# Where TensorE sums the values and turns the probabilities in the dilated attention of a two-block kernel

## The chip, the cores and the metric

The kernel runs on one core of one Trainium2 chip. The metric is device time in microseconds (us) of one execution, as the median of several runs. Engines are named as in the profile: PE is TensorE (matmuls and transposes), PEld its weight load, DVE is VectorE, ACT is ScalarE, POOL is GpSimd, SP is SyncE, which issues the weight loads from memory.

## What is computed

Two transformer blocks on 512 tokens of width 1024, in f32. Only the first block's attention is touched by the change. It is a dilated attention of 12 heads of 64 channels, beside a pooling branch of 256 channels:

```python
for window, dilation in ((128, 1), (512, 4), (2048, 16)):
    o, lse = dilated_branch(q, k, v, window, dilation)
w = softmax(stack(lses)); attn = sum(w * outs)
pool = (mean of the last 2, 4, 8 or 16 tokens - u) @ w_pool * pool_scale
x = x + rms_norm(concat([pool, attn]) @ w_out)
```

The kernel computes the three branches as one causal softmax: a bias table holds the logarithm of the number of branches that see a key, so each head needs one matrix of scores, one of probabilities and one product with the values. Queries and keys are rotated (rope) first.

## The kernel before

All activations are held with channels on partitions and the 512 tokens along the free axis. A weight tile of 128 output channels is a **unit**. It is used in three products: the weights are split into a high part WH (copied by ACT, `split_hi`, line 336) and a low part WL (subtracted by POOL, line 595), the input into HH and HL. `high_part` (lines 355 and 356) issues 8 x 2 matmuls of 128x512, WH with HH and with HL. `low_part` (line 364) issues 8 more, WL with HH. These run in a rounded f32 format; scores, turns and values are plain f32 matmuls.

The heads are taken in six pairs. `attn_stage(j, a)` on each engine does the projections of pair j (units u, u+1, u+2: queries, keys, values) and the attention of pair a = j - 1; the last call has no j and takes the first units of the output projection (`some_out`, lines 391 to 393) in the place of the projections. "The stage of pair a" means this call. Every engine runs its instructions in the order in which they are written, and they meet through semaphores. The order on PE in the stage of pair a, before the change:

- `scores()`, line 900: 8 matmuls into banks 2 to 6. Waits for the rotated queries and keys of the pair (`a_qk`) and, for a > 0, for all copies of turned probabilities of pair a-1 (`a_pt_act`, `a_pt_dve`).
- `turn_v()`, line 940: 4 transposes of the pair's values into bank 1.
- the first unit into bank 0 (`high_part`, `low_part`).
- `values(a - 1)`, line 931: 8 matmuls of probabilities with values of the pair before into bank 7.
- the second unit into bank 1.
- `turn(0)`, line 916: 10 transposes of head 0's probabilities PR into banks 2, 3 and 4, which signal three times.
- `high_part` of the third unit, which waits for the pair j's rotated queries (`a_qk`, since it writes bank 0).
- `turn(1)`: the same for head 1 into banks 5, 6 and 4. It waits until DVE has copied both of head 0's pieces (`a_pt_dve`), since both heads use bank 4.
- `low_part` of the third unit, and in the stages of pairs 1 and 3 (`POOL_ENDS`) `pool_product`, line 879, which waits for the pooling differences DF of DVE (`p_d`).

What stands on the other engines, in order, is not touched. On DVE: mask head 0, mask head 1 (line 2181), normalise head 0 (2190, 2194), the query's cosine product (2145), normalise head 1, the query's rotation (2149, 2153), the low half of the mixed values (2165), in pairs 1 to 3 two running sums of the pooling (2115), and then

```python
                    times_cos(1)
                if a is not None and j is not None:
                    copy_probs(0)
                ...
                    if a in POOL_ENDS:
                        pool_averages(POOL_ENDS[a])
                    rotate(1)
                    if a in POOL_ENDS:
                        pool_differences(POOL_ENDS[a])
                if a is not None:
                    copy_probs(1)
                if j is not None:
                    scale_v()
```

`copy_probs(h)` takes two pieces of a head out of the banks (lines 2201 and 2203), `pool_averages` is line 2130, `pool_differences` line 2133, `scale_v` line 2159. On ACT: `copy_v` (1596, waits for `turn_v`), the exponentials of head 0 (1576), the split of unit u+2, the exponentials of head 1, four copies that swap the query's halves (1584), the high half of the mixed values (1569), the split of u+3, the swap of the key's halves, head 0's third piece (1591), the split of u+4, head 1's third piece, and in pairs 1 and 3 the scaled pooling result. POOL makes the low weights of the next unit as soon as an old one is done.

Of the kernel before, what the change touches and what calls it, by code (L numbers as in the profile page):

```python
# [76 lines left out]
def t_width(block):  # L77
    return T - P * block


def s_width(block):
    return P * (block + 1)
# [46 lines left out]
def build(nc, ins, out_t):  # L129
    ctx = ExitStack()  # L130
    with ctx:
# [127 lines left out]
        POOL_ENDS = {1: 0, 3: 1}  # L259
# [88 lines left out]
        def high_part(pe, u, bank, chunks, xh, xl, k0=0, start=True, halfway=None, at=DC // 2):  # L348

            wh = WH[u.s]  # L350
            pe.wait_ge(s_hi, u.index + 1)
            for c in range(chunks):
                if halfway is not None and c == at:
                    halfway()
                pe.matmul(bank, wh[:, c, :], xh[:, k0 + c, :], start=(start and c == 0), stop=False)  # L355
                mm = pe.matmul(bank, wh[:, c, :], xl[:, k0 + c, :], start=False, stop=False)  # L356
            mm.then_inc(s_hi_used, 1)

        def low_part(pe, u, bank, chunks, xh, k0=0, stop=True):

            wl = WL[u.s]
            pe.wait_ge(s_lo, u.index + 1)
            for c in range(chunks):
                mm = pe.matmul(bank, wl[:, c, :], xh[:, k0 + c, :], start=False,  # L364
                               stop=(stop and c == chunks - 1))
            mm.then_inc(s_unit, 1)
# [284 lines left out]
        def _(pe):  # L651
            def mean_of_sum(n):

                if n == 0:
                    pe.wait_ge(s_sq_used, DC)
                    pe.matmul(B[7][:], MEAN[:], ACC[:], start=True, stop=True).then_inc(s_mean, 1)
                    return

                pe.wait_ge(s_mean_r, 1)
                pe.wait_ge(s_sum_lo, MEANS[n] - 1)  # L660
                pe.matmul(B[7][:], MEANR[:], ACCH[:], start=True, stop=False)
                pe.matmul(B[7][:], MEANR[:], ACCL[:], start=False, stop=True).then_inc(s_mean, 1)
# [198 lines left out]
            def some_out(b, which):  # L861

                if 0 in which:

                    if b == 0:
                        pe.wait_ge(a_vs, PAIRS1)
                    else:
                        pe.wait_ge(a_v, PAIRS1)
                some_chunks(pe, Unit(U_OUT1 + b), B[b][:], which, M1H, M1L, ready_m1)

            def finish_out(b):
                finish_unit(pe, Unit(U_OUT1 + b), B[b][:], DC, M1H, M1L, ready_m1)

            def pool_product(t):

                pe.wait_ge(p_d, t + 1)

                pe.wait_ge(s_m, PAIR_DONE[2 * t])
                pe.matmul(B[7][:], WPOOL[:, t, :], DF[:, t, :], start=True, stop=True).then_inc(p_y, 1)

            def attn_stage(j, a):

                u = None if j is None else Unit(U_ATTN + 3 * j)
                first = j == 0
                first_a = a == 0
                ap = None if a is None else a % 2

                def scores():

                    pe.wait_ge(a_qk, a * 2 + 2)  # L890
                    if not first_a:
                        pe.wait_ge(a_pt_act, a * 2)
                        pe.wait_ge(a_pt_dve, a * 4)
                    for h, tb, bank, at in ((0, 1, 4, 0), (1, 3, 5, 0), (0, 3, 2, 0), (1, 2, 6, 0), (0, 2, 3, 0),
                                            (1, 1, 4, 256), (0, 0, 3, 384), (1, 0, 6, 384)):
                        w = s_width(tb)
                        r = slice(64 * h, 64 * h + 64)
                        if h == 1 and bank == 4:
                            pe.wait_ge(a_scores, a * 8 + 1)
                        pe.matmul(B[bank][:, at:at + w], QT1[r, ap, P * tb:P * tb + P], KT1[r, ap, 0:w],  # L900
                                  start=True, stop=True).then_inc(a_scores, 1)

                def turn(h):
                    hd = a * 2 + h
                    pe.wait_ge(a_probs, hd * 4 + 4)
                    if h == 0:
                        pe.wait_ge(a_masked, a * 8 + 8)
                    else:
                        pe.wait_ge(a_pt_dve, hd * 2)
                    full, rest = ((2, 3), (5, 6))[h]  # L910
                    for blocks in (((0, full, 0),), ((1, rest, 0), (3, rest, 384)), ((2, 4, 256 * h),)):
                        for sb_, bank, at in blocks:
                            for tb in range(sb_, TB):
                                col = S_AT[tb] + P * sb_
                                o = at + P * (tb - sb_)
                                mm = pe.transpose(B[bank][:, o:o + P], PR[:, h, col:col + P], IDENT[:])
                        mm.then_inc(a_turned, 1)

                def values(a, ap):

                    pe.wait_ge(a_pt_act, a * 2 + 2)
                    pe.wait_ge(a_pt_dve, a * 4 + 4)
                    pe.wait_ge(a_v, a + 1)
                    if a in POOL_ENDS:
                        pe.wait_ge(p_yt, POOL_ENDS[a] + 1)
                    elif a:
                        pe.wait_ge(s_m, PAIR_DONE[a - 1])
                    for sb_ in range(TB):
                        w = t_width(sb_)
                        for h in range(2):  # L930
                            mm = pe.matmul(B[7][64 * h:64 * h + 64, P * sb_:T], VN1[:, ap, sb_, 64 * h:64 * h + 64],  # L931
                                           PT[:, h, T_AT[sb_]:T_AT[sb_] + w], start=(sb_ == 0),
                                           stop=(sb_ == TB - 1), skip_group_check=True)
                    mm.then_inc(a_pv, 1)

                def turn_v():
                    pe.wait_ge(a_vs, a + 1)
                    pe.wait_ge(a_qk, a * 2 + 2)
                    for tb in range(TB):
                        mm = pe.transpose(B[1][:, P * tb:P * tb + P], V1[:, P * tb:P * tb + P], IDENT[:])  # L940
                    mm.then_inc(a_vt, 1)

                if a is not None:
                    scores()
                    turn_v()
                if j is not None:
                    if not first:
                        pe.wait_ge(a_vs, j)
                    high_part(pe, u, B[0][:], DC, HH, HL)
                    if first:  # L950
                        pe.wait_ge(s_const, 16 * N_CONST)
                        mean_of_sum(0)
                    low_part(pe, u, B[0][:], DC, HH)
                if a is not None:
                    if not first_a:
                        values(a - 1, 1 - ap)
                    if j is None:
                        some_out(0, range(0, 5))
                        turn(0)
                        some_out(0, range(5, 6))  # L960
                        some_out(1, range(0, 1))
                        turn(1)
                        some_out(0, range(6, 7))
                        some_out(1, range(1, 2))
                        values(a, ap)
                        some_out(1, range(2, 5))
                        finish_out(0)
                        some_out(1, range(5, 7))
                        finish_out(1)
                if j is not None:  # L970
                    if not first:
                        pe.wait_ge(a_v, j)
                    use_unit(pe, u + 1, B[1][:], DC, HH, HL)
                    if a is not None:
                        turn(0)
                    pe.wait_ge(a_qk, j * 2 + 1)
                    high_part(pe, u + 2, B[0][:], DC, HH, HL)
                    if a is not None:
                        turn(1)
                    low_part(pe, u + 2, B[0][:], DC, HH)  # L980
                    if a in POOL_ENDS:
                        pool_product(POOL_ENDS[a])
# [25 lines left out]
            for j in range(1, PAIRS1):  # L1008
                attn_stage(j, j - 1)
            attn_stage(None, PAIRS1 - 1)  # L1010


# [1626 lines left out]
```

## Time and profile before

| | before |
|---|---|
| median of 3 runs | 1965.98 us (1965.83 to 1966.38) |
| span of the profiled execution | 1964.0 us |
| PE busy | 1957.2 us, 100% of the span |
| DVE busy | 865.8 us, 44% |
| ACT busy | 801.4 us, 41% |
| POOL busy | 764.9 us, 39% |
| granted clock of TensorE, mean | 1.000 |

The profile's span ends with the last instruction; the median of the runs is 2.0 us longer. The attention of the first block lies between about 37 and 173 us. A row of the timeline gives the start in us, the busy time in us, the engine, the line, the operation, what it writes and reads, and how many instructions are merged in it; in brackets stands the idle time before it and what ended that. Consecutive matmuls overlap in the records, so how long a group holds PE is read from its start to the start of what follows.

### The profile page before, as it was taken

How to read it: one execution, taken by the hardware profiler on the slowest of the kernel's cores; microseconds unless marked ns; L12 is line 12 of the kernel's file. 1: busy time of each engine (PE TensorE's matmuls, PEld its weight loads, DVE VectorE, ACT ScalarE, POOL GpSimd, SP SyncE). 2: the span in 40 equal slices, each digit the busy share in tenths (PEclk: the TensorE clock that was granted, in tenths of full speed). 3: DMA queues.
4: the chain of work that ended last, by engine and by line, in shares of the span. 5: the costliest groups of instructions: out<-in, count | busy, mean ns of one | idle time of the engine just before them, and what ended most of it. 6: DMA issues, size and time to landing. Idle time of an engine off the chain costs nothing.

```text
span 1964.0 us, 25749 instructions
## 1 busy us (share of the span) xinstructions
PE 1957.2 (100%) x8959; PEld 1590.7 (81%) x8959; DVE 865.8 (44%) x1148; ACT 801.4 (41%) x1078; POOL 764.9 (39%) x307
## 2 busy tenths in 40 slices
PE   9999999999999999999999999999999999999999
PEld 6777888888888778787888888888777788888887
DVE  5775653433145335333243434224788763433200
ACT  6665533233243433324332223225888752323211
POOL 4223344444413334243444444443222244444443
PEclk9999999999999999999999999999999999999999
DMA  5212122223223222222232223222111122222332
GB/s 172 75 65 86 65 97 96 96 96 115 91 74 123 70 86 91 69 87 85 86 105 98 96 96 102 99 99 85 54 63 46 63 97 96 96 96 96 110 97 93
DMA packets 49013, 177.39 MB, mean 90 GB/s; under 512 B 5569, under 2 KB 6465, under 8 KB 48961
## 3 DMA queue, kind: packets, MB, share of 16 engines
q1 hardware_dynamic: 46656, 172.95, 26.3%
q10 hardware_dynamic: 2304, 3.74, 0.6%
q8 instruction: 34, 0.56, 0.1%
q14 instruction: 19, 0.15, 0.0%
HBM read 174.57 MB, written 2.10 MB: 90 GB/s over the span
## 4 chain that ended last, share of the span: by engine, by line
PE 98%; DVE 1%; ACT 0%; DMA 0%; issue 0%; SPq 0%; DVEq 0%; ACTq 0%
PE B L355 26%; PE B L356 26%; PE B L364 26%; PE B L1114 2%; PE B L1251 2%; PE B L1072 1%; PE B L1076 1%; PE B L1073 1%; PE B L381 1%; PE B L377 1%; PE B L376 1%; PE B L1240 1%; PE B L1296 1%; PE B L1158 1%; PE B L900 1%; PE B L931 1%
## 5 line engine op out<-in xcount | busy, mean ns | idle before, releaser
L595 POOL TENSOR_TENSOR WL<-RAW,WH 128x1024 fp32r<-128x1024 f32 (+1 forms) x296 | 753.9, 2549 | 1171.5 <-PE B L364 763.8
L355 PE MATMUL B<-HH,WH 128*128 128x512 f32 x1608 | 629.1, 391 | 0.3 <-DVE QT L2153 0.3
L356 PE MATMUL B<-HL,WH 128*128 128x512 f32 x1608 | 626.1, 389 | 0.0
L336 ACT CAST WH<-RAW 128x1024 fp32r<-128x1024 f32 (+1 forms) x300 | 329.1, 1098 | 555.6 <-PE B L356 475.0
L364 PE MATMUL B<-HH,WL 128*128 128x512 f32 x1608 | 398.3, 390 | 0.0
L355 PEld LDWEIGHTS B<-HH,WH 128*128 128x128 f32 x1608 | 301.8, 188 | 64.9 <-issue 1.7
L364 PEld LDWEIGHTS B<-HH,WL 128*128 128x128 f32 x1608 | 301.4, 188 | 63.2 <-POOL WL L595 0.4
L356 PEld LDWEIGHTS B<-HL,WH 128*128 128x128 f32 x1608 | 301.9, 188 | 62.4
L1921 DVE TENSOR_TENSOR U<-B,RB 128x512 f32<-128x512 f32 x66 | 45.6, 691 | 294.3 <-PE B L364 294.3
L355 PE MATMUL B<-MH,WH 128*128 128x512 f32 x440 | 171.2, 389 | 0.0
L356 PE MATMUL B<-ML,WH 128*128 128x512 f32 x440 | 171.2, 389 | 0.0
L1924 DVE TENSOR_TENSOR HD<-SG,U 128x512 f32<-128x512 f32 x66 | 148.7, 2253 | 7.4 <-ACT SG L1414 0.7
L1418 ACT CAST MH<-HD 128x512 f32 (+1 forms) x66 | 41.0, 621 | 247.0 <-DVE HD L1924 247.0
L1904 DVE TENSOR_TENSOR ACC<-ACC,SQ 128x512 f32<-128x512 f32 x38 | 75.0, 1973 | 114.9 <-ACT SQ L1392 114.8
L1939 DVE TENSOR_TENSOR X<-X,B 128x512 f32 x26 | 17.9, 687 | 216.0 <-PE B L364 195.5
L364 PE MATMUL B<-MH,WL 128*128 128x512 f32 x429 | 103.6, 389 | 0.0
L356 PEld LDWEIGHTS B<-ML,WH 128*128 128x128 f32 x440 | 82.6, 188 | 17.2
L355 PEld LDWEIGHTS B<-MH,WH 128*128 128x128 f32 x440 | 82.6, 188 | 17.1
L364 PEld LDWEIGHTS B<-MH,WL 128*128 128x128 f32 x429 | 80.5, 188 | 16.7
L1414 ACT ACTIVATE SG<-G 128x512 f32<-128x512 f32 x66 | 41.8, 633 | 87.6 <-DVE G L1919 87.6
L1927 DVE TENSOR_TENSOR ML<-HD,MH 128x512 f32 (+1 forms) x66 | 49.4, 748 | 58.3 <-ACT MH L1418 58.3
L1919 DVE TENSOR_TENSOR G<-B,RB 128x512 f32<-128x512 f32 x66 | 45.6, 691 | 54.5 <-PE B L364 45.9
(377 smaller groups left out, 2257.9 us busy)
## 6 DMA issues: line engine op xcount, KB each, us to landing
RAW<-in_w_small SPq DMA_DIRECT2D x254, 512.0 KB, 3.3
RAW<-in_w_large SPq DMA_DIRECT2D x48, 704.0 KB, 4.1
out_t<-X SPq DMA_DIRECT2D x7, 256.0 KB, 5.2
X<-in_x_t ACTq DMA_DIRECT2D x4, 256.0 KB, 6.2
X<-in_x_t SPq DMA_DIRECT2D x4, 256.0 KB, 6.5
DECAY<-in_decay ACTq DMA_DIRECT2D x4, 256.0 KB, 2.6
RAW<-in_w_small ACTq DMA_DIRECT2D x2, 256.0 KB, 6.5
RAW<-in_w_small SPq DMA_DIRECT2D x2, 256.0 KB, 7.4
```

The source lines that it names most:

```text
L336: act.copy(wh, raw).then_inc(s_hi, 1)
L355: pe.matmul(bank, wh[:, c, :], xh[:, k0 + c, :], start=(start and c == 0), stop=False)
L356: mm = pe.matmul(bank, wh[:, c, :], xl[:, k0 + c, :], start=False, stop=False)
L364: mm = pe.matmul(bank, wl[:, c, :], xh[:, k0 + c, :], start=False, stop=(stop and c == chunks - 1))
L595: pool.tensor_tensor(wl, raw, wh.bitcast(F32), ALU.subtract).then_inc(s_lo, 1)
L1414: act.activation(SG[:], G1[:], ACT.Silu).then_inc(s_silu, 1)
L1418: act.copy(MH[:, i, :], HD[:]).then_inc(s_m_hi, 1)
L1904: dve.tensor_tensor(ACC[:], ACC[:], SQ[b][:], ALU.add).then_inc(s_sq_used, 1)
L1919: dve.tensor_tensor(G1[:], gate, RB[:], ALU.mult).then_inc(s_gate, 1)
L1921: dve.tensor_tensor(U1[:], up, RB[:], ALU.mult).then_inc(s_up, 1)
L1924: dve.tensor_tensor(HD[:], SG[:], U1[:], ALU.mult).then_inc(s_hidden, 1)
L1927: dve.tensor_tensor(ML[:, i, :], HD[:], MH[:, i, :].bitcast(F32), ALU.subtract).then_inc(s_m, 1)
```

## The change

Two groups of PE instructions move; none is added or removed, and no other engine's order changes. In the stages of pairs 1, 3 and 5, `values(a - 1)` moves from behind the first unit (in pair 5's stage: from behind `turn_v`) to directly behind `scores()`. In pairs 2 and 4 it stays, since there bank 7 holds the pooling product. And in the stages of pairs 0 to 4 `turn(0)` moves from ahead of the third unit's high part to behind it, directly ahead of `turn(1)`.

```diff
+                values_late = a is not None and a - 1 in POOL_ENDS
                 if a is not None:
                     scores()
+                    if not first_a and not values_late:
+                        values(a - 1, 1 - ap)
                     turn_v()
...
                 if a is not None:
-                    if not first_a:
+                    if values_late:
                         values(a - 1, 1 - ap)
...
                     use_unit(pe, u + 1, B[1][:], DC, HH, HL)
-                    if a is not None:
-                        turn(0)
                     pe.wait_ge(a_qk, j * 2 + 1)
                     high_part(pe, u + 2, B[0][:], DC, HH, HL)
                     if a is not None:
+                        turn(0)
                         turn(1)
                     low_part(pe, u + 2, B[0][:], DC, HH)
```

The turns, on PE in the stage of pair 0: L364 is the low part of the second or third unit, L355 and L356 the high part of the third, L916 a turn. Before:

```order
L364 MATMUL B<-HH,WL 128x512 x7
L916 MATMUL B<-IDENT,PR 128x128 [waits a_scores_masked,a_probs_ready]
L916 MATMUL B<-IDENT,PR 128x128 x9
L355 MATMUL B<-HH,WH 128x512 [waits weights_hi,a_qk_ready]
L356 MATMUL B<-HL,WH 128x512
...
L916 MATMUL B<-IDENT,PR 128x128 [waits a_probs_copied_vector,a_probs_ready]
L916 MATMUL B<-IDENT,PR 128x128 x9
L364 MATMUL B<-HH,WL 128x512 [waits weights_lo]
```

The same place now:

```order
L355 MATMUL B<-HH,WH 128x512
L356 MATMUL B<-HL,WH 128x512
L916 MATMUL B<-IDENT,PR 128x128 [waits a_scores_masked,a_probs_ready]
L916 MATMUL B<-IDENT,PR 128x128 x9
L916 MATMUL B<-IDENT,PR 128x128 [waits a_probs_copied_vector,a_probs_ready]
L916 MATMUL B<-IDENT,PR 128x128 x9
L364 MATMUL B<-HH,WL 128x512 [waits weights_lo]
L364 MATMUL B<-HH,WL 128x512 x7
```

The first turn has moved past the 16 matmuls of the high part, and the second turn with its wait for DVE's copies stands right behind it.

The values, on PE in the stage of pair 1: L900 are scores, L940 the turn of the values, L931 the values of pair 0. Before:

```order
L900 MATMUL B<-KT,QT 128x256 [waits a_scores_ready]
L900 MATMUL B<-KT,QT 128x128 x2
L940 MATMUL B<-IDENT,V 128x128 [waits a_qk_ready,a_v_scaled]
L940 MATMUL B<-IDENT,V 128x128 x3
L355 MATMUL B<-HH,WH 128x512 [waits weights_hi,a_v_scaled]
L356 MATMUL B<-HL,WH 128x512
```

And now:

```order
L900 MATMUL B<-KT,QT 128x128 x2
L931 MATMUL B<-PT,VN 64x512 [waits a_v_ready,a_probs_copied_vector,a_probs_copied_scalar]
L931 MATMUL B<-PT,VN 64x512
L931 MATMUL B<-PT,VN 64x384 x2
L931 MATMUL B<-PT,VN 64x256 x2
L931 MATMUL B<-PT,VN 64x128 x2
L940 MATMUL B<-IDENT,V 128x128 [waits a_qk_ready,a_v_scaled]
L940 MATMUL B<-IDENT,V 128x128 x3
```

The values have moved up past the first unit, and the turn of the next pair's values now stands behind them.

## Rows read from the trace of the kernel before

**Rows 1.** The page's part 1: busy time, share of the span, instructions.

```profile
PE 1957.2 (100%) x8959; PEld 1590.7 (81%) x8959; DVE 865.8 (44%) x1148; ACT 801.4 (41%) x1078; POOL 764.9 (39%) x307
```

**Rows 2.** Busy time by stretch: length, PE, PEld, DVE, ACT, POOL, clock, DMA.

```profile
36.00:182.00 146.00, 145.97 (x771) 112.16 (x770) 98.06 (x252) 88.17 (x187) 42.72 (x18) 1.00 0.19 63
```

**Rows 3.** Timeline of PE, stage of pair 0, from the second unit's low part.

```profile
49.34 1.98 PE L364 MATMUL B<-HH,WL 128*128 128x512 f32 x8
51.16 1.26 PE L916 MATMUL B<-IDENT,PR 128*128 128x128 f32 x10
52.18 0.47 PE L355 MATMUL B<-HH,WH 128*128 128x512 f32 x1
...
55.93 1.25 PE L916 MATMUL B<-IDENT,PR 128*128 128x128 f32 x10
56.94 2.09 PE L364 MATMUL B<-HH,WL 128*128 128x512 f32 x8
58.96 2.43 PE L900 MATMUL B<-KT,QT 64*128 64x256 f32 x16
```

**Rows 4.** Timeline of PE around its one wait for the rotation, before pair 0's stage.

```profile
31.72 0.50 PE L355 MATMUL B<-HH,WH 128*128 128x512 f32 x1 [0.25 <-DVE QT L2153]
32.06 0.39 PE L356 MATMUL B<-HL,WH 128*128 128x512 f32 x1
```

**Rows 5.** Timeline of DVE: query rotations' ends, and copies of pair 0's head 1.

```profile
30.97 0.69 DVE L2153 TENSOR_TENSOR QT<-RT 128x512 f32<-128x512 f32 x1
...
50.90 0.69 DVE L2153 TENSOR_TENSOR QT<-RT 128x512 f32<-128x512 f32 x1
...
56.57 0.69 DVE L2201 COPY PT<-B 128x512 f32<-128x512 f32 x1 [0.30 <-PE B L916]
57.22 0.42 DVE L2203 COPY PT<-B 128x256 f32<-128x256 f32 x1
```

**Rows 6.** Timeline of PE, stage of pair 1: first unit's low part, values, pooling product.

```profile
65.45 1.98 PE L364 MATMUL B<-HH,WL 128*128 128x512 f32 x8
67.36 2.37 PE L931 MATMUL B<-PT,VN 128*64 128x512 f32 x16
...
82.97 1.02 PE L879 MATMUL B<-DF,WPOOL 128*128 128x512 f32 x2
```

**Rows 7.** Timelines of DVE, POOL and ACT, stage of pair 1.

```profile
72.12 0.69 DVE L2153 TENSOR_TENSOR QT<-RT 128x512 f32<-128x512 f32 x1
...
77.03 1.45 DVE L2130 TENSOR_TENSOR DF<-WA,INV 64x512 f32<-64x512 f32 x1
...
80.57 0.68 DVE L2133 TENSOR_TENSOR DF<-DF,UP 128x512 f32<-128x512 f32 x1
...
75.55 2.39 POOL L595 TENSOR_TENSOR WL<-RAW,WH 128x1024 fp32r<-128x1024 f32 x1 [5.66 <-PE B L364]
...
76.22 2.39 ACT L1584 COPY QC<-B 32x512 f32<-32x512 f32 x4 [1.49 <-DVE RT L2145]
```

**Rows 8.** Timelines of PE, ACT and DVE, stage of pair 5.

```profile
159.48 0.66 PE L940 MATMUL B<-IDENT,V 128*128 128x128 f32 x4
160.07 2.37 PE L931 MATMUL B<-PT,VN 128*64 128x512 f32 x16
...
165.91 1.25 PE L916 MATMUL B<-IDENT,PR 128*128 128x128 f32 x10
...
168.39 1.25 PE L916 MATMUL B<-IDENT,PR 128*128 128x128 f32 x10
...
160.17 0.59 ACT L1596 COPY VN<-B 128x512 f32<-128x512 f32 x1 [4.30 <-PE B L940]
161.13 0.40 ACT L1576 ACTIVATE PR<-PR,NM 128x128 f32<-128x128 f32 x1 [0.38 <-DVE NM L2185]
...
163.67 1.27 DVE L2194 TENSOR_SCALAR PR<-PR,RD 128x128 f32<-128x128 f32 x4
...
167.64 0.42 DVE L2203 COPY PT<-B 128x256 f32<-128x256 f32 x1
```

## The prediction

> **What bounds the kernel now.** I read the page's busy shares first: PE is busy for 1957.2 of 1964.0 us [rows 1], no other engine for half. Then the stretches by time: between 36 and 182 us, where all of the change lies, PE is idle for 0.03 us of 146, at a granted clock of 1.00 [rows 2]. So PE in its written order is the bound, every other engine catches up inside each stage, and the change can act in two ways only: it can make the same instructions pack more tightly, or it can make PE wait where it never waited. The third view is the timeline, engine by engine, which gives both prices. The reader is to see in it what each wait of a moved instruction is waiting for, and how long ago that was done.
>
> **What tighter packing could give.** The instruction count is the same. A low part of 8 matmuls takes 51.16 - 49.34 = 1.82 us, 0.2275 us each [rows 3]. The 16 of a high part behind a turn take 55.93 - 52.18 = 3.75 us, where 16 x 0.2275 is 3.64: leaving plain f32 for the rounded format costs 0.11 us. Entering a turn costs nothing (that same low part, followed by one, shows 1.82). Entering the values costs 67.36 - 65.45 - 1.82 = 0.09 us [rows 6]. So putting two turns together saves one exit, 0.11 us, five times: 0.55 us. Values behind scores save an entry and an exit, 0.20 us, but they are a seam of their own kind: in pair 5's stage 4 transposes followed by values take 0.59 us [rows 8], while by the turn's 1.02 us for 10 they should take 0.41. That costs 0.18. I take the moved values as worth 0, with -0.2 to +0.2 us for each of the three stages as bounds.
>
> The Trainium skill (TensorE: Matmul & The Clock Gate, Part 2, step 5) states that the next matmul is issued before the last has drained, so that a stream's spacing is set by its columns alone. By that rule a seam costs nothing and merging would save nothing, and the sum below would be 0.55 us higher. The rows show 0.11 us at each exit, and I go by the rows.
>
> **The wait between the two turns.** The second turn waits for DVE's two copies of head 0. Until now the third unit's high part, 3.75 us, hid them. Now nothing does. How long they take behind a turn is seen at head 1 of pair 0, where DVE was idle and waiting: the turn starts at 55.93 [rows 3], the copies run from 56.57 to 57.22 + 0.42 = 57.64 [rows 5], 1.71 us behind its start. From a DVE end to PE's start are 0.06 us (30.97 + 0.69 = 31.66 to 31.72), and the first matmul after a wait takes 0.34 us instead of 0.23, 0.11 more [rows 4]. The first turn itself takes 56.94 - 55.93 = 1.01 us. So PE waits 1.71 + 0.06 - 1.01 = 0.76 us, plus 0.11 for the restart, less the 0.11 saved at the seam: **0.76 us in each of five stages, 3.8 us**. Bounds: without restart cost 0.65, with a DVE that comes 0.15 us late 0.91; 3.2 to 4.6 us.
>
> **The rotation of the query.** The third unit's high part waits for it, and now starts without the first turn ahead. In pair 0's stage it could start at 51.16, but the rotation ends at 50.90 + 0.69, and reaches PE at 51.65 [rows 3, 5]: a wait of 0.49 us and 0.11 for the restart, **0.6 us**. In the stages of pairs 1 and 3 the values too have left their place between the units. There the rotation comes through ACT's queue, which takes up again when the first unit's high part ends: 65.45 to 72.12 + 0.69 + 0.06 = 72.87, that is 7.42 us later [rows 6, 7]. PE now has 1.82 + 3.64 + 1.82 = 7.28 us of work in between: a wait of 0.14, with restart 0.25, **0.5 us in both stages** (0 to 1.0). This holds if the values' later turn doesn't push ACT: its copy starts 0.69 us behind the turn's start and takes 0.59, and the exponentials and DVE's reciprocal 163.67 - 161.13 = 2.54 [rows 8], 3.8 us together; from the turn's start to the end of the high part are 0.41 + 3.75 = 4.16. It is covered, with 0.3 us to spare. In pairs 2 and 4 the values (2.3 us) stay between the units and cover the rotation: 0.
>
> **The pooling product, pairs 1 and 3.** DVE runs in order, and behind head 0's copies stand two averages, the key's rotation and the differences, for which PE's product waits. Let U be the start of the high part. PE: first turn U + 3.64, second at + 1.77, then 0.11, 1.01 and the low part, 2.02 less the 0.09 of entering scores: product due at U + 8.5. DVE: the rotation ended at U, then the low half, two sums and the cosine product, 4 operations of 0.6 to 0.7 us; if undisturbed the copies end at U + 5.35, two averages (0.7 each, the 0.68 of the differences' row being the nearest) at 6.75, rotation 8.1, differences 8.8, a wait of 0.35 us. But an average that took 1.45 us at 77.03 ran under POOL's weight subtraction, 75.55 to 77.94 [rows 7], about 0.75 us more than its like; now the sums fall under one. They then end up to 2 us later, ACT's swap of the key (2.39 us) ends at about U + 7, and the differences at U + 9.1: a wait of 0.6 us. I take 0.6 + 0.11 = 0.7, **1.4 us for the two** (0 to 2.4). The product itself takes about 1 us [rows 6] and covers head 1's copies, which come behind the differences.
>
> **The last stage, pair 5.** No projection stands there to cover anything. Values go ahead of the turn of V and take 2.3 us (busy 2.37), so ACT's copy starts at 162.47 instead of 160.17 and ends at 163.06; the exponentials, which started at 161.13, come 1.9 us later. Head 0's probabilities were ready at 163.67 + 1.27 = 164.94, for a turn at 165.91 [rows 8]: 1 us of slack. Now they are ready for PE at 166.9, 1.0 us late. The copies that the second turn waits for ended at 167.64 + 0.42 = 168.06; 1.9 and 0.06 later is 170.0, where the turn stood at 168.39: 1.6 us late in all, and 0.11 for a restart: **1.7 us** (1.2 to 2.1).
>
> **Sum.** 3.8 + 0.6 + 0.5 + 1.4 + 1.7 + 0 = 8.0 us. PE is the bound to the end, so nothing behind it gives this back: span 1964.0 + 8.0 = 1972.0, and since the runs' median lies 2.0 us above the span, **1974.0 us**, 0.4% slower. All low ends together give +3.2 + 0.5 + 0 + 0 + 1.2 - 0.6 = +4.3, all high ends +4.6 + 0.7 + 1.0 + 2.4 + 2.1 + 0.6 = +11.4.
>
> **Rivals.**
> *Only the wait between the turns is real*: the other engines, busy below half, pull the rest forward, and rotation, product and last stage cost little. For it: DVE and ACT idle in each stage. Against: in the rows above each late thing hangs on a chain from PE's own signal. 3.8 + at most 0.6, about 1970.2.
> *Not slower*: PE does not stand still between the turns. That decides at one place: if head 0's copies reached PE within 1.0 us of the first turn's start, the wait would be gone, and 5 x 0.11 us of seams plus 3 x 0.2 of moved values would be left, 1964.8, no change. For it only that the first turn signals three times, so that copying begins before it ends; against it the 1.71 us of [rows 3, 5], the same operations on an idle DVE. The same time comes if the change's waits were already covered, which the orders of the section on the change exclude.
> *More*: POOL blocks DVE in the product's stages for averages and sums both, and ACT's pieces of the probabilities, behind the key's swap and a weight split, hold the next scores too: another 1 to 1.5 us in two stages, 1976.5 to 1977.
> *The clock*: it stays at 1.00 through all scores and turns now [rows 2]. If two turns with a pause, 2.8 us in one piece, made it fall to 1.2 of 2.4 GHz, the low part and the scores behind, 2.02 and 2.4 us, would take twice as long, 4.4 us in five stages, 22 us: 1996. In the Trainium skill, TensorE: Matmul & The Clock Gate, Part 4, transposes are said not to count as activity for the gate, which speaks for it; that scores and four transposes in a row, now, leave the clock alone speaks against it.
>
> **Chances.** Forecast 0.80 (1971 to 1977), only the turns' wait 0.08, not slower 0.05, more 0.06, clock 0.01. The two small cases above the forecast and the one with no change leave out 0.12 if the range reaches down to the second case's edge: 1970.6 to 1976.8. A measurement of this kernel tells about 0.2%, 3.9 us, from no change, that is 1969.9. Slower by more: 0.90, nearly all of the forecast, the larger cases and part of the second; within: 0.08; faster by more: 0.02, since no term gives 3.9 us.
>
> **What would show it.** In the changed kernel's timeline PE shows idle of about 0.75 us ended by DVE's copies ahead of the second L916 group, five times; an idle of 0.5 us ended by the rotation ahead of L355 in pair 0's stage and 0.1 to 0.2 in pairs 1 and 3; one of 0.3 to 0.7 us ahead of L879, twice; two, 1.1 and 0.5 us, in pair 5's stage. PE's idle time between 36 and 190 us should be 6 to 8 us, where it was 0.03. The forecast is wrong if that idle is under 3 us, if the seams between formats turn out several tenths dearer than the records show (their ends are modelled), or if PE is later held by something that now also comes late.

## The result and the profile after

The changed kernel takes 1973.76 us, the median of 5 runs (1973.44 to 1973.96), against 1965.98 us before (1965.81 to 1966.38). The ratio is 1.0039, with a 95% interval of 1.0028 to 1.0051: it is slower by 7.8 us. The forecast was 1974.0 us, with a range from 1970.6 to 1976.8.

The first view is the page's part 1 of the changed kernel, and under it the busy times by stretch, as in [rows 1] and [rows 2].

```profile
span 1971.7 us, 25749 instructions
...
PE 1960.2 (99%) x8959; PEld 1590.9 (81%) x8959; DVE 868.1 (44%) x1148; ACT 800.3 (41%) x1078; POOL 764.9 (39%) x307
```

```profile
36.00:190.00 154.00, 148.02 (x772) 112.09 (x771) 100.21 (x252) 87.44 (x187) 43.09 (x18) 1.00 0.18 60
```

The span has grown by 7.7 us. In the 154 us from 36 us on, PE is idle for 5.98 us, where it was idle for 0.03 us of 146; the clock stays at 1.00. The timeline of PE names each of these idle times in brackets. These are those of pairs 0, 1, 2 and 5; pair 3 shows pair 1's two again (0.62 and 0.33 us) and pair 4 one of 0.62:

```profile
51.66 0.50 PE L355 MATMUL B<-HH,WH 128*128 128x512 f32 x1 [0.33 <-DVE QT L2155]
...
57.29 1.28 PE L916 MATMUL B<-IDENT,PR 128*128 128x128 f32 x10 [0.61 <-DVE PT L2205]
...
82.23 1.28 PE L916 MATMUL B<-IDENT,PR 128*128 128x128 f32 x10 [0.62 <-DVE PT L2205]
...
85.70 1.13 PE L879 MATMUL B<-DF,WPOOL 128*128 128x512 f32 x2 [0.33 <-DVE DF L2135]
...
108.92 1.28 PE L916 MATMUL B<-IDENT,PR 128*128 128x128 f32 x10 [1.01 <-DVE PT L2205]
...
172.99 1.31 PE L916 MATMUL B<-IDENT,PR 128*128 128x128 f32 x10 [0.97 <-DVE PR L2196]
...
176.20 1.28 PE L916 MATMUL B<-IDENT,PR 128*128 128x128 f32 x10 [0.50 <-DVE PT L2205]
```

Of the forecast waits these show five between the two turns (0.61 to 1.01 us), the rotation in pair 0, two for the pooling product and two in pair 5's stage. Their sum, 5.9 us, stands at the low edge of the 6 to 8 us that the forecast named, because a record's modelled end reaches into what follows: 0.16 us for a low part, 0.24 us for a turn. For the same reason the rotation's small waits in pairs 1 and 3 have no bracket. They show from start to start:

```profile
74.57 1.98 PE L364 MATMUL B<-HH,WL 128*128 128x512 f32 x8
76.55 0.50 PE L355 MATMUL B<-HH,WH 128*128 128x512 f32 x1
```

The low part takes 1.98 us up to the next start, for 1.81 us where nothing waits, and the first matmul behind it 0.34 us (76.55 to 76.89) for 0.23. So the cost is better read from start to start. The table gives each stage as the time from its first scores to the next stage's first scores (for pair 5 to the last values, line 931), for all kernels of this study. In the kernel before, the scores start at 37.39, 58.96, 83.92, 108.02, 133.02 and 157.12 us, the last values at 170.97.

| kernel | pair 0 | 1 | 2 | 3 | 4 | 5 | median us |
|---|---|---|---|---|---|---|---|
| before | 21.57 | 24.96 | 24.10 | 25.00 | 24.10 | 13.85 | 1965.98 |
| after | 22.93 | 26.43 | 25.24 | 26.42 | 24.86 | 15.53 | 1973.76 |
| turns_only | 22.94 | 26.12 | 25.23 | 26.13 | 24.88 | 13.87 | 1971.52 |
| values_only | 21.58 | 26.41 | 24.11 | 26.42 | 24.11 | 15.52 | 1970.76 |
| wait_at_bank4 | 22.19 | 26.43 | 24.45 | 26.45 | 24.06 | 14.98 | 1970.73 |
| pair5_undone | 22.98 | 26.41 | 25.28 | 26.42 | 24.88 | 13.87 | 1972.24 |
| values_1_3 | 21.57 | 26.41 | 24.11 | 26.42 | 24.11 | 13.83 | 1968.67 |
| values13_sums | 21.58 | 24.70 | 24.09 | 24.74 | 24.08 | 13.83 | 1965.40 |
| pool_early | 22.96 | 25.87 | 24.85 | 25.82 | 24.87 | 15.52 | 1972.18 |
| copies_twice | 23.44 | 26.65 | 25.34 | 26.65 | 25.31 | 15.51 | 1975.17 |
| all_covered | 22.16 | 24.98 | 24.05 | 24.99 | 24.06 | 13.85 | 1966.39 |
| best2 | 21.58 | 24.70 | 24.42 | 24.74 | 24.03 | 13.85 | 1965.64 |

After against before, the six stages are longer by 1.36, 1.47, 1.14, 1.42, 0.76 and 1.68 us, 7.8 us in all: the whole difference. Nothing behind the attention gives any of it back.

### The profile page after: what moved, and what is told of

It reads as the page before. It is cut to its first block, busy times and chain, and to the rows that moved or that the text cites. A ratio compares the mean times of both kernels' runs of the same rounds, so it can differ in the third digit from the quotient of the medians.

```text
span 1971.7 us, 25749 instructions
## 1 busy us (share of the span) xinstructions
PE 1960.2 (99%) x8959; PEld 1590.9 (81%) x8959; DVE 868.1 (44%) x1148; ACT 800.3 (41%) x1078; POOL 764.9 (39%) x307
## 4 chain that ended last, share of the span: by engine, by line
PE 95%; DVE 2%; ACT 2%; issue 1%; DMA 0%; SPq 0%; DVEq 0%; ACTq 0%
PE B L355 25%; PE B L356 25%; PE B L364 25%; PE B L1116 2%; PE B L1253 2%; PE B L1074 1%; PE B L1078 1%; PE B L1075 1%; PE B L376 1%; PE B L377 1%; PE B L381 1%; PE B L1242 1%; PE B L1298 1%; PE B L1160 1%; PE B L900 1%; PE B L931 1%
## 5 line engine op out<-in xcount | busy, mean ns | idle before, releaser
L355 PE MATMUL B<-HH,WH 128*128 128x512 f32 x1608 | 628.6, 391 | 0.5 <-DVE QT L2155 0.3
L356 PE MATMUL B<-HL,WH 128*128 128x512 f32 x1608 | 626.1, 389 | 0.0
L364 PE MATMUL B<-HH,WL 128*128 128x512 f32 x1608 | 398.4, 390 | 0.0
L355 PEld LDWEIGHTS B<-HH,WH 128*128 128x128 f32 x1608 | 301.8, 188 | 66.0 <-DVE QT L2155 2.1
L364 PEld LDWEIGHTS B<-HH,WL 128*128 128x128 f32 x1608 | 301.4, 188 | 63.1 <-POOL WL L595 0.4
L356 PEld LDWEIGHTS B<-HL,WH 128*128 128x128 f32 x1608 | 301.9, 188 | 62.5
L355 PE MATMUL B<-MH,WH 128*128 128x512 f32 x440 | 171.2, 389 | 0.0
L356 PE MATMUL B<-ML,WH 128*128 128x512 f32 x440 | 171.2, 389 | 0.0
L364 PE MATMUL B<-MH,WL 128*128 128x512 f32 x429 | 103.6, 389 | 0.0
L355 PEld LDWEIGHTS B<-MH,WH 128*128 128x128 f32 x440 | 82.6, 188 | 17.2
L356 PEld LDWEIGHTS B<-ML,WH 128*128 128x128 f32 x440 | 82.6, 188 | 17.1
L364 PEld LDWEIGHTS B<-MH,WL 128*128 128x128 f32 x429 | 80.5, 188 | 16.7
```

## The experiments

**One part at a time.** The first two kernels do one part of the change each.

turns_only leaves the values where they were:

```diff
-                values_late = a is not None and a - 1 in POOL_ENDS
+                values_late = a is not None and not first_a
...
-                    if values_late:
+                    if not first_a:
                         values(a - 1, 1 - ap)
```

> The changed kernel with the values back behind the first unit in every stage; only the first turn is moved behind the third unit's high part. If the seven waits are as priced: pair 0's stage 1.4 us longer than in the kernel before (rotation 0.5, turns 0.6, two restarts), pairs 2 and 4 0.8 each, pairs 1 and 3 1.2 each (the pooling product 0.3 us late), pair 5 unchanged: +5.3 us, 1971.3. Rival, in which the early values cause the cost and the turns little: within 1 us of the kernel before.

Measured 1971.52 us, a ratio of 1.0028 (1.0017 to 1.0038). The stages are 1.4 us longer in pair 0, 1.2 and 1.1 in pairs 1 and 3, 0.8 in pair 4, 1.1 in pair 2, as expected but for pair 2 (0.8). The turns alone cost 5.5 us.

values_only puts the first turn back:

```diff
                     use_unit(pe, u + 1, B[1][:], DC, HH, HL)
+                    if a is not None:
+                        turn(0)
                     pe.wait_ge(a_qk, j * 2 + 1)
                     high_part(pe, u + 2, B[0][:], DC, HH, HL)
                     if a is not None:
-                        turn(0)
                         turn(1)
```

> The changed kernel with the first turn back ahead of the third unit's high part; only the values are moved, in the stages of pairs 1, 3 and 5. If the waits are as priced: no wait in pairs 1 and 3, which get 0.2 us shorter each by two saved changes between plain f32 and the rounded format; pair 5's stage 1.7 us longer (waits of 1.0 and 0.5 us ahead of its two turns): +1.3 us, 1967.3. Rival, in which moved values cost at each place: pairs 1 and 3 longer too, +3 us or more.

Measured 1970.76 us, 1.0029 (1.0020 to 1.0038), 3.5 us above the expectation. Pair 5 is as expected, 1.7 us longer. But pairs 1 and 3 are 1.4 us longer each, where they should have become shorter: the rival of this run's expectation, +3 us or more, is what came. PE's timeline in pair 1's stage shows two waits, with the high part still between the turns:

```profile
75.47 1.25 PE L916 MATMUL B<-IDENT,PR 128*128 128x128 f32 x10
...
81.25 1.28 PE L916 MATMUL B<-IDENT,PR 128*128 128x128 f32 x10 [0.87 <-DVE PT L2206]
...
84.76 1.13 PE L879 MATMUL B<-DF,WPOOL 128*128 128x512 f32 x2 [0.38 <-DVE DF L2136]
```

The second turn waits for copies that the 3.75 us of the high part had always covered. DVE and POOL in the same kernel say why:

```profile
76.09 2.63 DVE L2118 TENSOR_TENSOR WA<-UP 128x512 f32<-128x512 f32 x1
78.75 0.69 DVE L2118 TENSOR_TENSOR WB<-WA 128x512 f32<-128x512 f32 x1
...
80.09 0.68 DVE L2204 COPY PT<-B 128x512 f32<-128x512 f32 x1
80.69 0.41 DVE L2206 COPY PT<-B 128x256 f32<-128x256 f32 x1
```

```profile
75.78 2.39 POOL L595 TENSOR_TENSOR WL<-RAW,WH 128x1024 fp32r<-128x1024 f32 x1 [3.10 <-ACT WH L336]
```

The first running sum takes 2.63 us, its twin behind it 0.69. POOL has begun its weight subtraction at 75.78, 0.3 us ahead of the sum, and ends at 78.17; the sum ends at 78.72, its own 0.69 us being what is left behind about 78.0. The head 0 copies stand behind both sums and start at 80.09, 4.6 us behind their turn. In the kernel before, the sums ran ahead of POOL's subtraction, which started at 75.55 [rows 7]:

```profile
73.33 0.68 DVE L2115 TENSOR_TENSOR WA<-UP 128x512 f32<-128x512 f32 x1
74.05 0.69 DVE L2115 TENSOR_TENSOR WB<-WA 128x512 f32<-128x512 f32 x1
```

The values' move has brought the query's rotation, and the sums behind it, 2.3 us later in the stage (15.5 us behind the scores' start for 13.2), right under it. The Trainium skill (SBUF — State Buffer, Who interferes with whom) states that a VectorE instruction with two SBUF inputs and a GpSimd one that reads SBUF exclude each other, and that the one that comes second stands still until the other is through; the 2.63 us beside 0.69 agree.

**Is it really the sums?** Two kernels without the turns' move and without pair 5's. values_1_3 moves the values in pairs 1 and 3 alone; values13_sums also moves the sums:

```diff
                     normalise(0)
+                if a in POOL_SUMS and j is not None:
+                    pool_sums(*POOL_SUMS[a])
                 if j is not None:
                     times_cos(0)
...
                 if j is not None:
-                    if a in POOL_SUMS:
-                        pool_sums(*POOL_SUMS[a])
                     times_cos(1)
```

> The kernel before, with the values moved behind the scores in pairs 1 and 3 only, the sums where they were. As the run with values alone showed in these two stages, 1.45 and 1.42 us more each: +2.9 us, 1968.9. If that run's cost there came from its other parts: no change.

> The kernel before, with the values moved behind the scores in pairs 1 and 3 only, and the vector engine's two running sums of the pooling moved from behind the query's rotation to behind the first head's normalisation, a place where POOL is not at work. If the early values cost by pushing those sums under POOL's weight subtraction, which the run with values alone suggests (its sum took 2.6 us for 0.7, and pairs 1 and 3 took 1.4 us more each): the cost goes and 0.2 us each are gained, 0.4 us less than the kernel before, 1965.6. Rival, in which the whole chain of the scalar engine is late, not the sums: 2 us or more above the kernel before.

Measured 1968.67 us, 1.0015 (1.0006 to 1.0024), and 1965.40 us, 0.9998 (0.9989 to 1.0007), against 1965.87 in this comparison. The two kernels differ in nothing but where two DVE instructions stand in each of three stages, and in time by 3.3 us. Both sums now take 0.69 us each, since they start before POOL does:

```profile
68.83 0.69 DVE L2118 TENSOR_TENSOR WA<-UP 128x512 f32<-128x512 f32 x1
69.56 0.69 DVE L2118 TENSOR_TENSOR WB<-WA 128x512 f32<-128x512 f32 x1
```

```profile
70.13 2.40 POOL L595 TENSOR_TENSOR WL<-RAW,WH 128x1024 fp32r<-128x1024 f32 x1 [8.29 <-PE B L364]
```

With that out of the way the stages of pairs 1 and 3 are 0.26 us shorter than before: this is what early values are worth where they cost nothing. It is too little for the runs' times to tell, though the stages show it.

**The wait between the turns.** wait_at_bank4 lets the second turn begin, and waits only where the shared bank is written:

```diff
-                    else:
-                        pe.wait_ge(a_pt_dve, hd * 2)
                     full, rest = ((2, 3), (5, 6))[h]
                     for blocks in (((0, full, 0),), ((1, rest, 0), (3, rest, 384)), ((2, 4, 256 * h),)):
+                        if h == 1 and blocks[0][1] == 4:
+                            pe.wait_ge(a_pt_dve, hd * 2)
```

> The changed kernel, but the second turn waits for the first head's copies only ahead of its last two transposes, the ones that write the bank both heads share; the 8 others go ahead. If the time between the turns is a wait for the vector engine's copies: it goes, 0.75 us and the restart of 0.1 in pairs 0, 2 and 4; in pairs 1 and 3 the pooling product's wait grows by the same amount, since the vector engine's chain behind the copies sets its time: 2.6 us less than the changed kernel, 1971.1. Rival, in which the product's wait is its own and short: 4.3 us less, 1969.4. Rival, in which the turns are slow for themselves: no change, 1973.8.

Measured 1970.73 us, 1.0025 (1.0016 to 1.0035), 3.0 us under the changed kernel. No second turn shows idle time any more. In pair 1 two turns now take 2.1 us, from 80.27 to 82.37. Pairs 0, 2 and 4 get 0.7 to 0.8 us shorter. Pairs 1 and 3 do not change at all, because the product waits longer instead:

```profile
80.27 2.34 PE L916 MATMUL B<-IDENT,PR 128*128 128x128 f32 x20
82.37 2.10 PE L364 MATMUL B<-HH,WL 128*128 128x512 f32 x8
85.61 1.13 PE L879 MATMUL B<-DF,WPOOL 128*128 128x512 f32 x2 [1.15 <-DVE DF L2135]
```

0.33 us have become 1.15. In these two stages DVE sets the time and PE's two waits are one debt, paid at either place. The 0.4 us beyond the expectation are pair 5's second turn, whose wait of 0.50 us falls to the same edit; I had not counted it.

**Doubling the copy.** copies_twice does one DVE copy of head 0 twice:

```diff
                     dve.wait_ge(a_turned, hd * 3 + 3)
+                    if h == 0 and j is not None:
+                        pstep(dve.tensor_copy(PT[:, h, 1024:1280], B[4][:, 256 * h:256 * h + 256]))
                     dve.tensor_copy(PT[:, h, 1024:1280], B[4][:, 256 * h:256 * h + 256]).then_inc(a_pt_dve, 1)
```

> The changed kernel, with the copy of the first head's last piece done twice on the vector engine in pairs 0 to 4 (one more operation of about 0.4 us with its completion, the first copy's result written over). If PE's wait between the turns and, in pairs 1 and 3, for the product are set by the vector engine's chain: each stage 0.4 us longer, +2.0 us, 1975.8. In pair 2 the copy has started 0.4 us late in every run with the turns together, with the vector engine idle; the added operation moves the place of its instructions, which tells whether that hangs on the place. Rival, in which the two turns are slow for themselves: no change.

Measured 1975.17 us, 1.0048 (1.0033 to 1.0064), 1.4 us more than the changed kernel and not 2.0. In pairs 0 and 4 the stage is 0.5 us longer and the wait 1.07 to 1.08 us where it was 0.61: the wait is DVE's chain, one for one. In pairs 1 and 3 it grows by the same, but the product's wait shrinks and the stage grows by only 0.2: in pair 1, from the start of the low part to the product are 2.24 us, for 2.43 in the changed kernel and 1.95 before. There the chain had 0.23 us of slack behind the averages, where it waited for ACT's swap of the key; the added copy falls partly into it. In pair 2 the stage grew by only 0.1, which is the next point.

**Pair 2's late copy.** The changed kernel's wait in pair 2 is 1.01 us, not 0.62. DVE, idle for 3.77 us, starts its copy 1.09 us behind the turn's start at 106.66; in copies_twice it is 0.71, with the turn at 107.29:

```profile
107.75 0.69 DVE L2203 COPY PT<-B 128x512 f32<-128x512 f32 x1 [3.77 <-PE B L916]
```

```profile
108.00 0.69 DVE L2203 COPY PT<-B 128x512 f32<-128x512 f32 x1 [3.00 <-PE B L916]
```

The first row is of the changed kernel, the second of copies_twice. Of the kernels with the turns together in pair 2, the copy is late by 0.4 us in after, turns_only, pair5_undone, wait_at_bank4 and best2, and on time in copies_twice, pool_early and all_covered. copies_twice has two more instructions ahead of it on DVE, the other two have the averages elsewhere; best2, where it is late, has only the sums elsewhere. pool_early differs from the changed kernel in DVE's order alone, so the delay hangs on what stands ahead in DVE's program and not on PE; what makes it no run shows, and it stays open. It is older than the change: in the kernel before, the copy starts at 101.31, 1.10 us behind its turn, and in values13_sums 1.10 us behind it too, after 0.20 us of an idle DVE. There the high part covered it.

**The pooling work out of the way.** pool_early is the changed kernel with the sums moved as above and the averages ahead of the copies:

```diff
                     times_cos(1)
+                    if a in POOL_ENDS:
+                        pool_averages(POOL_ENDS[a])
                 if a is not None and j is not None:
                     copy_probs(0)
...
-                    if a in POOL_ENDS:
-                        pool_averages(POOL_ENDS[a])
                     rotate(1)
```

> The changed kernel, with the vector engine's running sums behind the first head's normalisation and its two averages ahead of the first head's copies. If in pairs 1 and 3 the vector engine's pooling work is what holds the product: its waits of 0.33 us and their restarts go, and the copies are ready a little sooner; the turns' wait of 0.62 us and the rotation's of about 0.2 stay: 1.0 us less than the changed kernel, 1972.7. Rival, in which the product waits for the key's swap and rotation and not for the pooling work: no change, 1973.8.

Measured 1972.18 us, 1.0035 (1.0021 to 1.0048), 1.6 us less than the changed kernel. The product's waits are gone: 0.56 and 0.60 us less in pairs 1 and 3. The expectation, 1.0 us less, had these and not pair 2. The other 0.4 us are pair 2's late copy, which has come in time.

**Pair 5 alone.** pair5_undone keeps the old order in the last stage:

```diff
-                values_late = a is not None and a - 1 in POOL_ENDS
+                values_late = a is not None and (a - 1 in POOL_ENDS or a == PAIRS1 - 1)
```

> The changed kernel with only pair 5's stage as before (values behind the turn of V). If that stage's two waits come from the values' later turn through the scalar engine: 1.7 us less than the changed kernel, 1972.1. Rival, in which pair 5's stage is longer because all engines arrive late from the stages ahead: no change, 1973.8.

Measured 1972.24 us, 1.0032 (1.0019 to 1.0044): 1.5 us less, and the stage takes 13.87 us again. In the changed kernel ACT's copy of the values comes 0.70 us behind the turn of V at 167.94, the exponentials follow without a pause, and the first turn finds its probabilities 1 us late:

```profile
168.64 0.59 ACT L1598 COPY VN<-B 128x512 f32<-128x512 f32 x1 [6.73 <-PE B L940]
...
169.12 0.40 ACT L1578 ACTIVATE PR<-PR,NM 128x128 f32<-128x128 f32 x1
```

**All waits covered.** all_covered keeps the change in pairs 0 to 4 and puts the three cures together: the later wait of wait_at_bank4, pair 5 as before, DVE's pooling work as in pool_early.

> The changed kernel with every wait but the rotation's covered again: the second turn waits only ahead of its last two transposes, pair 5's stage is as before, the running sums stand behind the first head's normalisation and the averages ahead of the copies. If the waits found so far are the whole cost: pair 0 keeps 0.6 us (rotation), pairs 1 and 3 keep 0.3 us of rotation against 0.3 us saved, pairs 2, 4 and 5 are as before: +0.6 us, 1966.5. If something else in the new order costs as well, the stages stay longer with no wait to show for it: 1968 or more.

Measured 1966.39 us, 1.0003 (0.9994 to 1.0012), against 1965.90. PE has one wait with a bracket left in the attention, for pair 0's rotation:

```profile
52.23 0.50 PE L355 MATMUL B<-HH,WH 128*128 128x512 f32 x1 [0.34 <-DVE QT L2155]
```

In pairs 1 and 3 the rotation's small wait is left as well, without a bracket: the low part takes 1.98 us to the next start, as in the changed kernel. Wait and restart cost 0.3 us a stage there, and the early values give 0.26 back, as the expectation had it. The stages differ from before by +0.59, +0.02, -0.05, -0.01, -0.04 and 0.00 us. So 7.3 of the 7.8 us go with two edits outside the change and pair 5's part of it undone, and the turns together gain under 0.1 us even where nothing waits (pairs 2 and 4).

best2 keeps only what is covered: the early values in pairs 1 and 3 with the sums moved, the turns together in pairs 2 and 4 only, and the later wait.

> The parts of the change whose waits are covered, and no other: values early in pairs 1 and 3 with the running sums moved, the two turns together only in pairs 2 and 4, with the later wait. If a change of format on PE costs about 0.1 us: 0.4 us less by the values and up to 0.2 by the turns than the kernel before, 1965.3. Rival, in which putting the turns together saves nothing because their 20 transposes end together with the copies they wait for: 1965.5.

Measured 1965.64 us, 1.0000 (0.9991 to 1.0009), against 1965.90. Pair 4's stage is 0.07 us shorter than before, pair 2's 0.3 us longer by the late copy. No version here is faster than the kernel before by what can be measured.

## Why the prediction was right

The time came out at 1973.76 us for 1974.0, and the mechanism was the one forecast: waits of PE, not denser matmuls. Point by point, with the expected size first:

- **Wait between the turns, 0.76 us a stage.** Right in pairs 0 and 4: the stage of pair 4, in which nothing else changed, is 0.76 us longer. Doubling the copy lengthened it and the later wait took it away. In pair 2 it cost 1.14, by a late start of DVE. The forecast took pair 0's copies for all stages; in the trace of before, pair 2's copy was late too (1.10 us behind its turn), but covered. The 0.76 itself holds two small terms that were off and cancel: in pair 0 PE starts 0.15 us behind the end of the copy (57.14 to 57.29) and not 0.06, and the turn that follows the wait takes 1.04 us for 1.01, a restart of 0.03 and not 0.11.
- **Rotation in pair 0, 0.6 us.** Right: pair 0's stage is 1.36 us longer, which is 0.76 and 0.60, and all_covered keeps 0.59 of it.
- **Pairs 1 and 3, 0.76 + 0.25 + 0.7 = 1.7 us each.** Measured 1.47 and 1.42, and the three waits are right. In pair 1, start to start and with restarts, the rotation costs 0.34 us (74.57 to 80.36 is 5.79 for 5.45), the turns 0.77 (80.36 to 83.27 is 2.91 for two turns of 1.01, less the 0.12 of the exit), the product 0.59 (83.27 to 86.76 is 3.49 for 2.90): 1.70 us. The sum under POOL's subtraction is there too, 2.63 us at 77.01, and the differences end at 85.64, 9.1 us behind the start of the high part, as forecast. What was mis-sized is the values' worth, 0 for about 0.25 us. But the terms are not the price of each part of the change: turns_only costs 1.1 to 1.2 us in these stages, values_only 1.4, both together 1.4 to 1.5, so undoing the turns alone saves next to nothing there. The two parts don't add, because both uncover the same DVE chain. The forecast named the sums under POOL's subtraction only for the product's wait; with the high part back between the turns they make head 0's copies late as well. That I missed in the expectation of values_only, where I expected 0.4 us of gain from these stages and got 2.9 us of loss.
- **Value of the early values, 0.** It is 0.26 us per stage where it is covered (values13_sums). The seam that I priced from pair 5's turn of V followed by values, 0.18 us, does not exist between scores and values, nor between values and the turn of V. The bounds of 0.2 us a stage were a little too narrow.
- **Pair 5, 1.7 us.** Right, 1.68, and gone when that stage alone is put back.
- **The rivals.** "Only the wait between the turns" would be 1970.2: the undone parts show each of the others real. "Not slower" needed copies within 1.0 us of the turn's start; PE found them ready 1.9 us behind it, 57.29 for a turn at 55.42. "More" did not come: in no kernel of this study does PE show idle time ahead of the next scores. The clock stayed at 1.00 in all kernels, with 2.9 us of turns and pause in one piece. The Trainium skill (TensorE: Matmul & The Clock Gate, Part 4) states that a transpose does not count as PE being busy in the way that a matmul does; at this length it cost nothing here.

That the total is off by only 0.2 us is in part luck, since the errors that are left cancel: pairs 1 and 3 were priced 0.5 us too high together, pair 2 0.4 us too low.

## What to carry to other kernels

Where PE is never idle, ask of each instruction that is moved what it covered: grouping two like pieces of work is worth under 0.1 us (turns) or 0.26 us (values) here, and putting the turns together takes away 3.75 us of cover from copies that need 0.8 of it. If such a group must wait for a shared buffer, put the wait ahead of the part that writes it, not ahead of the group. And follow a delayed instruction onto the other engines: the values, moved up on PE, made the first unit that they moved past, and ACT's and DVE's work that waits for it, 2.3 us later, and so brought a DVE addition under a POOL instruction. That alone cost 1.4 us a stage (values_1_3) and stands nowhere in the diff.

## What the runs showed of the hardware

- A DVE addition of two SBUF tiles of 128x512 takes 0.69 us; started 0.3 us behind a POOL subtraction of 2.39 us it takes 2.63 us. A product with one input in PSUM (the key's cosine product in pair 0 of the changed kernel, at 51.71), started 0.3 us behind one of 2.45 us, took 0.69 us and was not held by it.
- Going from plain f32 matmuls to the rounded format costs PE about 0.11 us. Between scores and values, scores and transposes, and from values to transposes, all plain f32, nothing was lost; from the 4 transposes of V to values it was 0.18 us (0.59 for 0.41).
- After a wait, the first matmul of a high part takes 0.34 us to the next start, for 0.23. A turn after a wait takes 1.04 us for 1.01.
- A DVE copy started 0.4 us late at one place of DVE's program, in the five kernels that show it with the turns together, and on time in three whose program ahead of it was different; the cause is open.
